# Feed-forward first matrix of a float32 model block: one 512-column product for high and low input, halves summed by VectorE

## What is computed

```python
# first block, layer 0 and 1: width 1024 -> 4096 -> 1024
hf = rms_norm(x, ffn_norm[layer])
x = x + jnp.square(jax.nn.relu(hf @ ffn_w1[layer])) @ ffn_w2[layer]

# second block: width 1024 -> 2816 -> 1024
def swiglu(h, w_gate, w_up, w_down):
    return (jax.nn.silu(h @ w_gate) * (h @ w_up)) @ w_down
```

## Time and profile before

| | us |
|---|---|
| three runs: median (lowest to highest) | 946.72 (944.18 to 947.25) |
| the profiled execution, own time | 946.89 |
| its span, first to last instruction | 944.8 |
| TensorE busy (share of the span) | 899.5 (95%) |
| VectorE busy | 559.5 (59%) |
| ScalarE busy | 451.6 (48%) |
| GpSimd busy | 43.8 (5%) |
| mean granted TensorE clock, share of full | 0.983 |

### The profile page before, as it was taken

One profiled execution on the slowest core, in us unless ns is written; L12 is line 12 of the kernel. 1 busy time (PEld: TensorE's weight loads), 2 busy tenths in 40 slices (PEclk: granted clock), 3 DMA queues, 4 the chain that ended last, 5 costly groups with the idle time before them and its releaser, 6 DMA issues.

```text
span 944.8 us, 14140 instructions
## 1 busy us (share of the span) xinstructions
PE 899.5 (95%) x5706; PEld 799.2 (85%) x5706; DVE 559.5 (59%) x729; ACT 451.6 (48%) x580; POOL 43.8 (5%) x90
## 2 busy tenths in 40 slices
PE   8987899999999989889999999989998899999997
PEld 8866789999999868568999999979986799999996
DVE  4698776555555648756555555565774645554554
ACT  5357346444444445855444444455554543443332
POOL 1030001000000021011000000010000100000000
PEclk9999999999999989999999999999997899999999
DMA  9364345655555253055655565546431446556541
GB/s 306 119 227 140 108 135 188 200 192 178 178 180 192 92 199 134 1 185 186 208 195 187 185 202 188 178 134 211 147 134 45 135 157 201 178 184 214 172 140 45
DMA packets 97528, 155.34 MB, mean 164 GB/s; under 512 B 4175, under 2 KB 72428, under 8 KB 97484
## 3 DMA queue, kind: packets, MB, share of 16 engines
q1 hardware_dynamic: 94924, 149.37, 48.3%
q0 software_dynamic: 1504, 5.28, 1.7%
q10 hardware_dynamic: 1056, 0.07, 0.1%
HBM read 153.63 MB, written 1.09 MB: 164 GB/s over the span
## 4 chain that ended last, share of the span: by engine, by line
PE 82%; DVE 9%; ACT 5%; issue 2%; SPq 1%; POOL 1%; DMA 0%; DVEq 0%; ACTq 0%
PE psum L1597 26%; PE psum L1598 26%; PE psum L1599 25%; DVE w_lo L1047 2%; DVE arena L1174 2%; ACT h_hi L689 1%; DVE h_lo L1072 1%; ACT w_hi L660 1%; PE psum L2068 1%; PE psum L1618 1%; DVE arena L1435 1%; ACT arena L898 1%; PE psum L2039 1%; PE psum L2109 1%; PE psum L2133 0%
## 5 line engine op out<-in xcount | busy, mean ns | idle before, releaser
L1597 PE MATMUL psum<-h_hi,w_hi 128*128 128x256 f32 x1072 | 307.1, 286 | 3.2 <-DVE h_lo L1072 1.7
L1598 PE MATMUL psum<-h_lo,w_hi 128*128 128x256 f32 x1072 | 304.0, 284 | 0.0
L1599 PE MATMUL psum<-h_hi,w_lo 128*128 128x256 f32 x1072 | 303.9, 283 | 0.0
L1047 DVE TENSOR_TENSOR w_lo<-raw,w_hi 128x2048 fp32r<-128x2048 f32 (+3 forms) x82 | 182.8, 2233 | 108.3 <-ACT w_hi L660 93.9
L1597 PEld LDWEIGHTS psum<-h_hi,w_hi 128*128 128x128 f32 x1072 | 206.2, 192 | 8.2 <-issue 5.5
L1598 PEld LDWEIGHTS psum<-h_lo,w_hi 128*128 128x128 f32 x1072 | 206.3, 192 | 1.5
L1599 PEld LDWEIGHTS psum<-h_hi,w_lo 128*128 128x128 f32 x1072 | 206.2, 192 | 0.0
L660 ACT ACTIVATE w_hi<-raw 128x2048 fp32r<-128x2048 f32 (+2 forms) x74 | 135.8, 1841 | 86.6 <-PE psum L1599 83.8
L1062 DVE TENSOR_TENSOR w_lo<-raw,w_hi 128x2048 fp32r<-128x2048 f32 x54 | 123.8, 2292 | 87.0 <-ACT w_hi L678 87.0
L678 ACT ACTIVATE w_hi<-raw 128x2048 fp32r<-128x2048 f32 x66 | 126.0, 1908 | 69.5 <-PE psum L1599 69.5
L1597 PE MATMUL psum<-w_hi,g_hi 128*128 128x512 f32 x368 | 144.7, 393 | 0.0
(11 more groups left out here) (232 smaller groups left out, 779.5 us busy)
## 6 DMA issues: line engine op xcount, KB each, us to landing
raw<-in_ffn_w SPq DMA_DIRECT2D x64, 1024.0 KB, 5.2
raw<-in_w_qkv SPq DMA_DIRECT2D x12, 1024.0 KB, 5.2
raw<-in_ab_w_in SPq DMA_DIRECT2D x11, 1024.0 KB, 5.5
raw<-in_w_gate SPq DMA_DIRECT2D x11, 1024.0 KB, 5.4
raw<-in_w_up SPq DMA_DIRECT2D x11, 1024.0 KB, 5.3
raw<-in_w_down SPq DMA_DIRECT2D x11, 1024.0 KB, 5.0
raw<-in_ab_w_out SPq DMA_DIRECT2D x4, 1024.0 KB, 4.9
raw<-in_c_w_out SPq DMA_DIRECT2D x4, 1024.0 KB, 5.1
```

The lines of the kernel that those rows point to most:

```text
L1047: ins = dve.tensor_tensor(dst, src, high, ALU.subtract)
L1597: pe.matmul(dst, stat[0], mov[0], start=first, stop=False, skip_group_check=shared)
L1598: pe.matmul(dst, stat[0], mov[1], start=False, stop=False, skip_group_check=shared)
L1599: return pe.matmul(dst, stat[1], mov[0], start=False, stop=last, skip_group_check=shared)
```

## The change

`h_hi` and `h_lo` become the two halves of one buffer `h_both`, so that for one row block the high and the low input lie side by side, 512 columns. In the feed-forwards' first matrices `stationary` is replaced by `stationary_both`: `w_hi` by both halves as one product of 512 columns, and `w_lo` by the high half, 256 columns, added to the first half of the same bank. Each half `f` has a bank of its own, so a piece takes two. VectorE adds the two halves of a bank (`tensor_reduce` over the view `sums_of`). The first piece of each ungated feed-forward (`stationary_seam`) keeps its form; its hidden part is copied out of PSUM. ScalarE's Relu and Square go: VectorE's `relu2` takes max(a, 0) times a, and ScalarE copies that to `g_hi`. The order on VectorE in the ungated feed-forward changes as the diff shows. Banks: 4 and 5 or 6 and 7 in turn for ungated chunks, 4 and 5 for every gate, 6 and 7 for every up; TensorE waits for `hid_in`, `gate_in` and `up_in` before it writes them anew. TensorE's loop body has six chunks in place of three; VectorE's chunks in the ungated feed-forward are written out without a loop.

```diff
-        h_hi = sb("h_hi", [P, KB, S], F32R)
-        h_lo = sb("h_lo", [P, KB, S], F32R)
+        h_both = sb("h_both", [P, KB, 2, S], F32R)
+        h_hi, h_lo = h_both[:, :, 0, :], h_both[:, :, 1, :]
...
+        def hidden_banks(c_mod):
+            return 4 + 2 * (c_mod % 2)
+
+        def sums_of(b):
+            return psum[:, b:b + 2, :].rearrange("p f (u t) -> p f t u", u=2)
...
# ScalarE, ungated
-                def hidden(c, r, n_w1):
-
-                    act.wait_ge(piece_used, n_w1 + 1)
-                    if not (isinstance(c, int) and c < 3):
-                        act.wait_ge(g_lo_ready, hb + c - 2)
-                    act.activation(g_act[:, r, :], bank(4 + r), ACT.Relu).then_inc(act_out, 1)
-                    act.wait_ge(act_out, hb + c + 1)
-                    act.activation(g_hi[:, r, :], g_act[:, r, :], ACT.Square).then_inc(g_hi_ready, 1)
+                def hidden(c, r):
+
+                    act.wait_ge(mul_out, hb + c + 1)
+                    act.activation(g_hi[:, r, :], g_mul[:, r, :], ACT.Copy).then_inc(g_hi_ready, 1)
...
# VectorE, ungated
+                def relu2(c, r):
+
+                    dve.wait_ge(hid_in, hb + c + 1)
+                    dve.scalar_tensor_tensor(out=g_mul[:, r, :], in0=g_act[:, r, :], scalar=0.0, in1=g_act[:, r, :],
+                                             op0=ALU.max, op1=ALU.mult).then_inc(mul_out, 1)
+
+                def hidden(c, b, n_w1):
+
+                    r = c % 3
+                    dve.wait_ge(piece_used, n_w1 + 1)
+                    dve.tensor_reduce(g_act[:, r, :].rearrange("p (f t) -> p f t", f=2), sums_of(b), AX.X, ALU.add)                        .then_inc(hid_in, 1)
+                    relu2(c, r)
+
+                def low(c, r):
+
                     dve.wait_ge(mul_out, hb + c + 1)
                     dve.wait_ge(g_hi_ready, hb + c + 1)
                     dve.tensor_tensor(g_lo[:, r, :], g_mul[:, r, :], g_hi[:, r, :], ALU.subtract)\
                         .then_inc(g_lo_ready, 1)
 
-                hidden(0, 0)
+                dve.wait_ge(piece_used, first + 1)
+                dve.tensor_copy(g_act[:, 0, :], bank(4)).then_inc(hid_in, 1)
+                relu2(0, 0)
                 lo(first + RING)
...
+                low(0, 0)
+
+                for c in range(1, FC):
+                    n = first + 2 * c - 1
+                    hidden(c, hidden_banks(c), n)
+                    lo(n + RING)
+                    low(c, c % 3)
+                    if c < FC - 1:
+                        lo(n + 1 + RING)
                 seam(stage, first + 2 * FC - 1, t_next, jobs)
...
# VectorE, gated
             def glu_scale(c, r, n_gate):
 
                 dve.wait_ge(piece_used, n_gate + 1)
-                dve.tensor_tensor(g_act[:, r, :].rearrange("p (f t) -> p f t", f=2),
-                                  bank(4 + 2 * r).rearrange("p (f t) -> p f t", f=2),
-                                  r_row[:, :].unsqueeze(1).to_broadcast([P, 2, S]), ALU.mult).then_inc(gate_scaled, 1)
+                gate = g_act[:, r, :].rearrange("p (f t) -> p f t", f=2)
+                dve.tensor_reduce(gate, sums_of(4), AX.X, ALU.add).then_inc(gate_in, 1)
+                dve.wait_ge(gate_in, c + 1)
+                dve.tensor_tensor(gate, gate, r_row[:, :].unsqueeze(1).to_broadcast([P, 2, S]), ALU.mult)\
+                    .then_inc(gate_scaled, 1)
 
             def glu_mul(c, r, n_up):
-                dve.wait_ge(act_out, hb + c + 1)
                 dve.wait_ge(piece_used, n_up + 1)
-                dve.tensor_tensor(g_mul[:, r, :], g_act[:, r, :], bank(5 + 2 * r), ALU.mult).then_inc(mul_out, 1)
+                dve.tensor_reduce(g_mul[:, r, :].rearrange("p (f t) -> p f t", f=2), sums_of(6), AX.X, ALU.add)                    .then_inc(up_in, 1)
+                dve.wait_ge(act_out, c + 1)
+                dve.wait_ge(up_in, c + 1)
+                dve.tensor_tensor(g_mul[:, r, :], g_act[:, r, :], g_mul[:, r, :], ALU.mult).then_inc(mul_out, 1)
...
# TensorE
+            def stationary_both(slot, b, t=None, between=None):
+
+
+                wh = w_hi[:, slot, :].rearrange("p (k c) -> p k c", k=KB)
+                wl = w_lo[:, slot, :].rearrange("p (k c) -> p k c", k=KB)
+                for f in range(2):
+                    for k in range(KB):
+                        if t is not None and f == 0 and k % 2 == 0:
+                            h_wait(t, k)
+                        cs = slice(f * P, (f + 1) * P)
+                        pe.matmul(bank(b + f), wh[:, k, cs], h_both[:, k, :, :].rearrange("p u s -> p (u s)"),
+                                  start=k == 0, stop=False, skip_group_check=True)
+                        ins = pe.matmul(bank(b + f)[:, 0:S], wl[:, k, cs], h_hi[:, k, :],
+                                        start=False, stop=k == KB - 1, skip_group_check=True)
+                    if between and f == 0:
+                        between()
+                ins.then_inc(piece_used, 1)
...
# TensorE, ungated chunk
-                    r1 = (j + 1) % 3
-                    split(n + 6 * i)
-                    if not (isinstance(c, int) and c < 2):
-                        pe.wait_ge(act_out, hb + c - 1)
-                    stationary(n % RING, t, 4 + r1)
-                    split(n + 1 + 6 * i)
+                    split(n + 12 * i)
+                    if not (isinstance(c, int) and c == 0):
+                        pe.wait_ge(hid_in, hb + c)
+                    stationary_both(n % RING, hidden_banks(j + 1))
+                    split(n + 1 + 12 * i)
                     pe.wait_ge(g_lo_ready, hb + c + 1)
                     out_piece(hidden_of(j % 3), (n + 1) % RING, isinstance(c, int) and c == 0)
...
# TensorE, gated
             def gate_up(c, r, n0, i):
+                begin = isinstance(c, int) and c == 0
                 split(n0 + 6 * i)
-                if not (isinstance(c, int) and c < 2):
-                    pe.wait_ge(gate_scaled, c - 1)
-                stationary(n0 % RING, T_GLU, 4 + 2 * r, isinstance(c, int) and c == 0)
+                if not begin:
+                    pe.wait_ge(gate_in, c)
+                stationary_both(n0 % RING, 4, T_GLU if begin else None)
                 split(n0 + 1 + 6 * i)
...
+                if not begin:
+                    pe.wait_ge(up_in, c)
+                stationary_both((n0 + 1) % RING, 6, None, (lambda: spread_row(2, 0)) if begin else None)
```

More of the change, by code:

```diff
@@ L345, in build @@
         mul_out = sem("mul_out")
+        hid_in = sem("hid_in")
+        gate_in = sem("gate_in")
+        up_in = sem("up_in")
         g_hi_ready = sem("g_hi_ready")
@@ L695, in mix_hi @@
                 act.wait_ge(pv, 4 * q + 4)
-                act.activation(mix_part(t, q, h_hi, g_hi), bank(b), ACT.Copy).then_inc(h_hi_ready, 1)
+                act.activation(mix_part(t, q, h_hi, g_hi), blocks(b), ACT.Copy).then_inc(h_hi_ready, 1)
             sums = [0]
@@ L835, in chunk @@
                     n = first + 1 + 2 * j
-                    hidden(c + 1, (j + 1) % 3, n + 6 * i)
+                    hidden(c + 1, (j + 1) % 3)
                     if isinstance(i, int):
@@ L1429, in mix_lo @@
                 dve.wait_ge(h_hi_ready, t_base(t) + q + 1)
-                dve.tensor_tensor(mix_part(t, q, h_lo, g_lo), bank(b), mix_part(t, q, h_hi, g_hi), ALU.subtract)\
+                dve.tensor_tensor(mix_part(t, q, h_lo, g_lo), blocks(b), mix_part(t, q, h_hi, g_hi), ALU.subtract)\
                     .then_inc(h_lo_ready, 1)
@@ L1604, in h_block @@
                 if t == T_2MIX:
-                    at = (k % 2) * S + tb * P
-                    return [mix_part(t, k // 2, a, b)[:, at:at + P] for a, b in ((h_hi, g_hi), (h_lo, g_lo))]
+                    return [mix_part(t, k // 2, a, b)[:, k % 2, tb * P:(tb + 1) * P]
+                            for a, b in ((h_hi, g_hi), (h_lo, g_lo))]
                 return h_hi[:, k, tb * P:(tb + 1) * P], h_lo[:, k, tb * P:(tb + 1) * P]
@@ L1939, in ffn @@
                     chunk(j, j, 0)
-                with pe.Fori(1, (FC - 1) // 3) as i:
-                    for j in range(3):
-                        chunk(3 * i + j, j, i)
+                with pe.Fori(0, (FC - 4) // 6) as i:
+                    for j in range(3, 9):
+                        chunk(6 * i + j, j, i)
                 n = first + 2 * FC - 1
@@ L2173, in gate_up @@
             def gate_up(c, r, n0, i):
+                begin = isinstance(c, int) and c == 0
                 split(n0 + 6 * i)
-                if not (isinstance(c, int) and c < 2):
-                    pe.wait_ge(gate_scaled, c - 1)
-                stationary(n0 % RING, T_GLU, 4 + 2 * r, isinstance(c, int) and c == 0)
+                if not begin:
+                    pe.wait_ge(gate_in, c)
+                stationary_both(n0 % RING, 4, T_GLU if begin else None)
                 split(n0 + 1 + 6 * i)
-                if isinstance(c, int) and c == 0:
```

(11 more changed lines are left out.)

12 lines of the change are left out of this document (6 added, 6 removed).

## The result

| | before | changed |
|---|---|---|
| runs, median (lowest to highest), us | 946.59 (944.18 to 947.25), 4 runs | 957.27 (953.81 to 960.04), 4 runs |
| profiled execution, own time, us | 946.89 | 960.04 |
| its span, us | 944.8 | 958.2 |
| TensorE busy, us (products) | 899.5 (5706) | 900.7 (4874) |
| VectorE busy, us | 559.5 | 619.6 |

The changed kernel is slower: ratio 1.0118, 95% interval 1.0091 to 1.0144. The forecast was 951.1 with a range of 943.5 to 961.5. The sign and the range held; the size was +4.2 where +10.7 was measured, and 957.3 lies outside the 949.7 to 953.5 that the forecast's main case gave itself.

What follows compares the result with a forecast made beforehand. The prediction took TensorE alone to bound the kernel. Products -9.8, ungated delays +9.1 and gated delays +4.9 made +4.2 us on the profiled 946.9, so 951.1, with a range of 943.5 to 961.5.

Steps and rivals of the forecast that it cites:

- the forecast's main case: Whole kernel: gains and waits as worked out give 951.1 us, own range 949.7 to 953.5, chance 0.47.
- The ungated waits: Start and end of each ungated feed-forward: TensorE waits for `low`, queued behind `lo`, 2.16 and 2.18 us, plus 0.11 each.
- The gated waits: Gated feed-forward: TensorE waits 0.3, 1.2 and 1.1 us at the start, 2.05 at the end before the slow product.
- The chain: Gated chunk: serial VectorE and ScalarE work from reduction to last split takes 15.6 us, hidden under TensorE's 16.6.
- The reduction: VectorE adding a bank's two halves, 1024 values from PSUM: 1.22 us, lower end 0.69, upper end 2.44.
- The products: First matrices on TensorE: merging takes a piece from 5.75 to 5.56 us, 9.8 saved together.
- Rival 5: First matrices: the merged product keeps the fixed part of both, 0.240 us instead of 0.2277; no gain, 961; chance 0.04.
- the rule on the Trainium skill's page TensorE: First matrices: spacing N/2.4 + 2.5 ns, so merging saves 2.1 us over 832 blocks; time 959; no separate chance.
- The clock: TensorE: one or two of eight new waits may lower the clock, 3.4 us each; 954 to 958; chance 0.12.
- The forecast's own sum: Whole kernel: -9.8 for products, +9.1 for ungated and +4.9 for gated delays, +4.2 us in all.

Runs made afterwards that it cites:

- e1_low_first: Changed kernel, but in the ungated feed-forwards VectorE computes `low` before the split `lo` of the later piece; 944.2 us, ratio 0.9987 to the kernel before.
- e7_twice: Changed kernel with each of the two reductions of a gated chunk done twice, the first into a spare buffer; 973.7 us in one run.
- e2_pairs: Changed kernel, but TensorE issues two 512-column products and then two 256-column ones instead of alternating; 954.6 us, ratio 1.0112 to the kernel before.
- e3_three: Changed kernel with the merged product taken apart into two, buffers and queue order kept; 962.9 us, ratio 1.0162 to the kernel before.
- e4_second_half: Changed kernel, but `w_lo` by the high input is added to the bank's second half; 958.8 us, ratio 1.0141 to the kernel before.
- e8_filled: Changed kernel with 16 small products on TensorE ahead of each of the four ungated waits for `g_lo`; 959.5 us, ratio 1.0153 to the kernel before.

## Why the prediction was right and where it was wrong

**The ungated waits: right.** Forecast were 2.16 and 2.18 us and a slow first product of 0.11 more, twice each. Measured are four waits, 8.1 us idle plus the delay until products flow; from the last product before to the first behind it 2.25 us at the start (0.12 of them its own) and 2.43 at the end (0.23 its own), and 0.08 for the slow one: 2.2 to 2.3 each. `e1_low_first` shows the named cause, the split queued before `low`.

**The gated waits: right in place, a little high in size.** Forecast: 0.3, 1.2 and 1.1 at the start, 2.05 at the end. Measured: 0.2, 0.9 and 0.9, and 1.9. The chain was forecast at 15.6 against a cover of 16.6; `e7_twice` gives 15.4 against 16.8.

**The reduction: right.** 1.22 us for the pair of banks, the row with as many values; the bounds of 0.69 and 2.44 were both far off.

**The products: the step that failed.** The text said "A piece of 16 blocks takes 5.56 in place of 5.75: 0.19 saved". The sum of the spacings of two uniform runs, 0.2277 + 0.120, was taken for the spacing of an alternation. A block takes 0.353 and a piece 5.64, 0.11 saved, so the gain is some 5.7 us, not 9.8. `e2_pairs` reaches the 5.56 with the same products in another order, `e3_three` shows 5.75 without the merge and with the new buffer, and `e4_second_half` excludes the half of the bank. Rival 5, at 0.04, doubted this very step and put the merged product at 0.240 with 0.120 beside it; measured are 0.236 and 0.117, between it and the forecast. The estimate that the prediction worked out from the rule on the Trainium skill's page TensorE: Matmul & The Clock Gate, section Back-to-back issue gap, N/2.4 + 2.5 ns, would have made the gain 2.1 us, 3.6 too little where the forecast had 4.1 too much; the measured 0.236 and 0.117 do not agree with its 0.216 and 0.109.

**The clock: a rival that came true beside the forecast.** It was given a chance of 0.12 as a case of its own, "one or two may tip it", at 3.4 us each. The new idle waits do it in part of the executions: over ten runs the changed kernel has a mean clock of 0.982 where the kernel before has 0.987. A time of 955 at a clock lower by 0.0045 loses about 4 us, an estimate, and filling the waits gave 3.7 back. A single stretch behind a wait costs 1.6 us, not 3.4: the price was read from a stretch of 7 us, and the new ones last 3.4. The forecast's own sum should have carried part of it as a term, since its four long waits were in every execution.

**The sum again:** products -5.7, ungated waits +8.9, gated waits and slow products +4.3, clock +3.4 to 4 make some +11, where 10.7 and, in the later runs, 11.8 (957.2 against 945.4) were measured. Of the 6.5 us between forecast and result the products are 4.1 and the clock some 4; the waits, forecast at 14.0 and measured at 13.2, take 0.8 back: 7.3 together, between the 6.5 and the 7.6 of the later runs. That the result lies in the 954 to 958 of the rival on the clock is in part luck: its sum had neither the 4.1 us of the products nor stretches of the right length.

## What to carry to other kernels

Where TensorE has been the bound without a gap, the first thing to ask of a new step on another engine is not its length but what stands before its result in that engine's queue, at the first and the last round of a loop, where one product and not two covers it: here four delays of some 2 us cost 12 to 13 us with the clock that fell, while of the 60 us of added VectorE work (619.6 against 559.5) TensorE felt nothing in the ungated parts once `low` stood first. A wait of 2 us on TensorE should be priced above 2, with the chance that the clock falls behind it. The spacing of products must be measured in the order in which they will be issued; try an order in twos before a merged product is given up.

## What the runs showed of the hardware that was not expected

- Alternating products of 512 and 256 columns with a weight load each take 0.353 us a pair; two and two 0.348; four and four 0.349. In runs of one size they take 0.2277 and 0.120, together 0.3475. The products of 512 columns right behind those of 256 are slow, 0.236 us on the mean in alternation and 0.229 to 0.233 in groups of two or four, against 0.227 in the midst of a run; the 256-column ones right behind 512 are quick, 0.115 to 0.117 on the mean against 0.120. The cause is open.
- Idle waits of about 2 us lower the mean granted clock from 0.987 to 0.982, and small products in their place restore it, at waits that are all but unchanged. Not every such wait does it: 8 of 24 have a stretch of 3.4 us at half clock right behind them.
- A float32 product of 128 columns shows as two passes of 0.112 us in the trace of `e8_filled`.
